# Twelve groups of experts for nine: by request, in pairs, the emptiest last

## What is computed

```
g_idx = argmax(h @ rg_w + rg_b)                      # one of 4 groups per token
e_sel = (h @ re_w + re_b)[group g_idx]               # 8 logits
top_p, top_i = top_k(softmax(e_sel), 2)              # 2 experts per token
hid = silu(h @ w_gate[e]) * (h @ w_up[e]) * combine  # 1024 -> 256
y  += hid @ w_down[e]                                # 256 -> 1024
x   = layer_norm(alpha * x + g2 * y)
```

## Time and profile before

| | us |
|---|---|
| runs shown | 1051.68, 1734.73, 1049.01 |
| median | 1051.68 |
| the profiled execution | 1051.29 |
| its span | 1049.2 |
| TensorE busy | 845.7 (81 %) |
| VectorE busy | 303.8 (29 %) |
| ScalarE busy | 176.7 (17 %) |
| moved from and to memory | 324.48 MB |

### The profile page before, as it was taken

The page is one execution under the profiler, slowest core; times in us unless marked ns, Lnnn a source line. Parts: engine busy times, 40 slices in busy tenths (PEclk is TensorE's granted clock), DMA queues, the critical chain, the costliest instruction groups (busy, mean ns, idle before and its releaser), DMA issues.

```text
span 1049.2 us, 13222 instructions
## 1 busy us (share of the span) xinstructions
PE 845.7 (81%) x5572; PEld 576.2 (55%) x5572; DVE 303.8 (29%) x674; ACT 176.7 (17%) x387; POOL 26.4 (3%) x50
## 2 busy tenths in 40 slices
PE   4899999998976985766649998998998599576572
PEld 1787757876853542322428886687886245232251
DVE  2111333222567121100052223232356712111015
ACT  2101323210122110100021033151002212010001
POOL 0200000000000000000010000000000000000000
PEclk9899999999979998877679999999998999888777
DMA  9947963586648999999995415676554899999991
GB/s 371 411 181 283 374 241 126 221 282 247 280 192 329 429 429 431 430 430 427 422 425 231 171 34 202 279 281 241 161 241 170 328 430 429 428 430 430 429 421 75
DMA packets 38519, 324.48 MB, mean 309 GB/s; under 512 B 4921, under 2 KB 5049, under 8 KB 9393
## 3 DMA queue, kind: packets, MB, share of 16 engines
q1 hardware_dynamic: 34816, 313.02, 72.5%
q0 software_dynamic: 3200, 9.09, 2.7%
q10 hardware_dynamic: 432, 1.40, 0.3%
HBM read 321.06 MB, written 2.42 MB: 308 GB/s over the span
## 4 chain that ended last, share of the span: by engine, by line
PE 66%; DMA 21%; DVE 6%; issue 3%; ACT 3%; SPq 1%; DVEq 0%; ACTq 0%
DMA expert_gate_up<-in_w_gu 19%; PE ps L852 13%; PE ps L734 9%; PE ps L760 6%; PE ps L1012 5%; PE ps L926 5%; PE ps L998 5%; PE ps L663 4%; PE ps L684 2%; DMA dense<-in_w_ada 2%; PE ps L873 2%; PE ps L822 2%; PE ps L963 2%; PE ps L704 2%; PE ps L953 2%
## 5 line engine op out<-in xcount | busy, mean ns | idle before, releaser
L852 PE MATMUL ps<-expert_gate_up,gathered_even 128*32 128x512 f32 x640 | 85.3, 692 | 48.8 <-DMA expert_gate_up<-in_w_gu 45.3
L734 PE MATMUL ps<-hT,dense 128*128 128x256 f32 x512 | 114.8, 383 | 0.0
L734 PEld LDWEIGHTS ps<-hT,dense 128*128 128x128 f32 x512 | 96.6, 191 | 15.7 <-issue 2.6
L852 PE MATMUL ps<-expert_gate_up,gathered_odd 128*32 128x512 f32 x512 | 65.2, 667 | 44.5 <-DMA expert_gate_up<-in_w_gu 44.5
L852 PEld LDWEIGHTS ps<-expert_gate_up,gathered_even 128*32 128x32 f32 x640 | 26.4, 126 | 104.1 <-issue 104.1
L760 PE MATMUL ps<-dense,hT 128*128 128x256 f32 (+1 forms) x320 | 68.1, 377 | 1.7 <-ACT hT L1124 1.7
L663 PE MATMUL ps<-dense,cond 128*32 128x256 f32 x768 | 56.0, 422 | 16.7 <-ACT cond L1217 12.3
L852 PEld LDWEIGHTS ps<-expert_gate_up,gathered_odd 128*32 128x32 f32 x512 | 20.3, 121 | 88.6 <-issue 88.6
L873 PE MATMUL ps<-expert_down,hiddenT 128*32 128x512 f32 x576 | 65.5, 594 | 2.3 <-ACT hiddenT L1188 2.3
L1585 DVE TENSOR_TENSOR hidden<-hidden,ps 128x256 f32<-128x256 f32 x18 | 7.6, 420 | 203.3 <-ACT hidden L1184 203.3
L760 PEld LDWEIGHTS ps<-dense,hT 128*128 128x128 f32 x320 | 59.9, 198 | 10.0 <-ACT hT L1124 2.5
(11 more groups left out here) (239 smaller groups left out, 1031.2 us busy)
## 6 DMA issues: line engine op xcount, KB each, us to landing
expert_gate_up<-in_w_gu SPq DMA_DIRECT2D x64, 2048.0 KB, 19.0
expert_down<-in_w_dn SPq DMA_DIRECT2D x64, 1024.0 KB, 21.2
dense<-in_w_ada SPq DMA_DIRECT2D x48, 1024.0 KB, 9.8
dense<-in_w_in SPq DMA_DIRECT2D x28, 1024.0 KB, 11.6
dense<-in_w_o SPq DMA_DIRECT2D x8, 1024.0 KB, 6.2
dense<-in_w_out SPq DMA_DIRECT2D x8, 1024.0 KB, 4.8
dense<-in_w_c SPq DMA_DIRECT2D x4, 1024.0 KB, 28.4
dense<-in_w_uq SPq DMA_DIRECT2D x4, 576.0 KB, 6.4
```

Source lines behind the costliest of these rows:

```text
L734: last = mm(b[:, m * 256:(m + 1) * 256], w[:, k, m * P:(m + 1) * P], hT[:, k, :], start=(k == 0), stop=(k == KD - 1))
L852: last = mm(ps[32 * j:32 * j + 32, bank, :], xg[n % 2][:, k, at_ + j * CAP:at_ + (j + 1) * CAP], w_gu[BUFFER[held[j]]][:, k, :], start=(k ...
```

## The change

- Twelve groups. Experts 0 to 3 go by request: group 0 has their slots for request 0, group 1 for request 1, each 32. Groups 2 to 7 take two experts each with 64 slots: 4 to 7 by number and the eight fullest of the sort. Groups 8 to 11 take the sixteen emptiest with 32 slots. Buffers 0 to 3 are therefore free after group 1.
- Group 0's input is gathered from the normalised tokens `xh2` in one float32 product and modulated on the way out (`gathered_first`); `gate_up` of groups 0 and 1 is cut into pieces of the inputs that stand between router, count and token transposes. Group 0 goes as far as its `down` and `scatter` before the loop.
- The sort is a small permutation matrix `perm` made from 64 rows; TensorE applies it (`order_experts`, `turn_route`, `sort_route`). The 24 by 24 grids are gone.
- `choose` and `place` of request 0 stand on VectorE ahead of the layer norm's second half of request 1.
- The down load of expert 5 is issued right behind its gate/up load.
- The branch to the extra rounds is behind group 9, with groups 10 and 11 to follow. The last group's `gate_up` is done in halves, two experts and then two.

```diff
-FIRST_OF = (0, 4, 8, 10, 12, 16, 20, 24, 28)
+TILES = ((0, 1, 2, 3), (0, 1, 2, 3), (4, 4, 5, 5), (6, 6, 7, 7), (8, 8, 9, 9), (10, 10, 11, 11), (12, 12, 13, 13),
+         (14, 14, 15, 15), (16, 17, 18, 19), (20, 21, 22, 23), (24, 25, 26, 27), (28, 29, 30, 31))
-GROUPS = 9
-SPLIT = 7
+GROUPS = 12
+SPLIT = 9
 ...
+                for e in (6, 7):
+                    main_load(l, e)
                 sp.wait_ge(order_ready, l + 1)
+                    for e in (8, 9):
+                        main_load(l, e, which[e - 8])
+                    for e in (6, 7):
+                        main_down(l, e)
+                    for e in (8, 9):
+                        main_down(l, e, which[e - 8])
+                for g in range(5, SPLIT + 1):
+                    next_experts(l, TILES[g][0], TILES[g][-1] + 1)
 ...
+                pe.wait_ge(*reached(m, "sel_ready", 1))
+                pe.wait_ge(xh2_ready, 2 * l + 1)
+                gather_first(m, 0)
+                ada(l, a0 + 3)
+                turn_hidden2(l, 1)
+                gate_up(m, None, 0, 4, range(0, 2))
                 router(l, 1)
+                gate_up(m, None, 0, 4, range(2, 4))
+                gate_up(m, None, 0, 4, range(4, 6))
+                count(l, 1)
+                gate_up(m, None, 0, 4, range(6, 8))
+                gather_first(m, 1)
+                evacuated(l, ("h2T", 1, 0), ("h2T", 1, 1), ("route", 1), ("count", 0), ("count", 1))
+                turn_tokens(l, 0)
+                gate_up(m, None, 1, 1, range(0, 4))
+                turn_group(m, 0, 0, 4)
+                totals(l)
+                gate_up(m, None, 1, 1, range(4, 8))
+                turn_tokens(l, 1)
+                select_T(m, 0, 5)
+                down(m, None, 0, 0, EARLY_BANK)
+                order_experts(l)
+                select_T(m, 1, 0)
+                scatter(m, 0, 0, True)
 ...
+                        if g == GROUPS - 1:
+                            gate_up(m, None, g, g % 2, held=(0, 1))
+                            gate_up(m, None, g, g % 2, held=(2, 3))
+                        if g != SPLIT + 1:
+                            scatter(m, g - 1, g - 1, g == 2)
+                    if g == 2:
+                        turn_route(l)
 ...
+                    if g == 2:
+                        sort_route(l)
+                        pe.wait_ge(sorted_ready, l + 1)
                     down(m, None, g, g)
```

More of the change, by code:

```diff
@@ L83, with experts, requests, scattered @@
 COLUMN_PARTS = {0: 0, 1: 1, 3: 2, 4: 3}
-def tiles(g):
-    a = FIRST_OF[g]
-    return [a, a, a + 1, a + 1] if g in PAIRS else list(range(a, a + EPI))
+def experts(g):
+    return sorted(set(TILES[g]))
+def requests(g):
+    return ((0,), (1,), (0, 1))[min(g, 2)]
+def scattered(g):
+    return g if g < 2 else 2 * (g - 1)
 def dense_ada(layer):
@@ L498, in main_down, with next_experts @@
                 down_load(l, M[l], e, which)
-            def four_experts(l, a):
+            def next_experts(l, first, end):
                 with ExitStack() as hold:
[L503 to L508, removed]
+                    which = [whose(hold, e) for e in range(first, end)]
+                    for e in range(first, end):
+                        main_load(l, e, which[e - first])
+                    for e in range(first, end):
+                        main_down(l, e, which[e - first])
             def extra_loads(l, r):
@@ L800, in gather_first @@
-            def gather_first(w, s):
[L802 to L810, removed]
+                        last = tr(ps[:, TOKEN_BANK[c], j * P:(j + 1) * P], h2T[:, s, 4 * c + j, :], ident)
@@ L812, in gather @@
+            def gather_first(w, s):
+                for f in range(2):
+                    for j in range(4):
+                        k = 4 * f + j
+                        last = mm(ps[:, FIRST_BANK[s][f], j * P:(j + 1) * P], xh2[:, s, k * P:(k + 1) * P],
+                                  sel[:, 0, s, 0:P].bitcast(F32), start=True, stop=True)
+                    last.then_inc(w["xg_filled"], 1)
             def gather(w, n, banks, evacs):
[L814 removed]
@@ L862, in turn_group, with down @@
                 last.then_inc(w["hidT_filled"], 1)
-            def down(w, r, done, g):
-                held = tiles(g)
-                for e in sorted(set(held)):
+            def down(w, r, done, g, banks=(2, 3)):
+                for e in experts(g):
                     pe.wait_ge(*reached(w, "dn_in", landed(r, e), BUFFER[e]))
@@ L1606, in extra_round @@
                 w = X[l]
-                first, end = PLACES_OF[WIDE]
-                for a, b, slots in ((0, first, CAP), (first, end, 2 * CAP), (end, NE, CAP)):
-                    last = V.tensor_scalar(posx[:, :, a:b], posx[:, :, a:b], -float(slots), None, ALU.add)
+                for n in range(CHUNKS):
+                    a, b = PLACES_OF[n]
+                    last = V.tensor_scalar(posx[:, :, a:b], posx[:, :, a:b], -float(SLOTS_OF[n]), None, ALU.add)
                 last.then_inc(w["round_ready"], 1)
@@ new lines, in _ @@
+                sort_experts(l)
+                weigh(l, 1)
+                select_T(m, 0, 0, 5)
+                hidden_product(m, 1, 1, 1)
+                bias_ada(7 if l == 0 else 11)
+                token_low(l, 1)
+                name_experts(l)
+                low(m, 0, 0, EARLY_BANK)
+                combine(l, 1)
+                select_T(m, 1, 1, 0)
+                select(m, 1, (0, 1))
+                if l == 0:
+                    columns(7)
+                for g in range(1, GROUPS):
+                    n = g // 2
+                    if g > 1:
+                        hidden_product(m, g, g, g % 2)
+                    if g == 2:
+                        turn_route(l)
+                    more = g % 2 and g < GROUPS - 1
+                    if more and g != SPLIT:
```

438 lines of the change are left out of this document (232 added, 206 removed).

## The result

The changed kernel takes 1061.77 us (median of 4 runs, 1060.09 to 1065.48), the kernel before 1051.62 (median of 4 beside it, one of which took 1734.73 us and stands alone). The ratio is 1.0107, 95 % interval 1.0079 to 1.0135: slower by 1.1 %, clear of no change, though by less than 2 %. 1062 was forecast. The profiled execution is the slowest of the four, 1065.48 with a span of 1063.5; before it was 1051.29 and 1049.2.

A forecast was written before the change was run, and what follows sets the result against it. TensorE was to bound the row of pair groups up to group 6, then memory after a dry queue. A later restart (3.1 us) and 203.6 us behind it gave +3.6 and +7.3 a layer: about 1062 us, range 1038 to 1077.

The forecast's parts named there:

- the sum: Both layers' expert stages added up: +3.6 us in the first, +7.3 in the second, together +10.9 on the profiled 1051.29.
- 44 MiB behind expert 18's buffer: Loads left at group 6's gate/up end, held by SP's in-order issue until its buffers are free: 107.3 us of memory time.
- The restart: Moment the expert loads resume after running dry; predicted at 328.1 us, 3.1 later than before, when group 1's gate/up ends.
- half clock: TensorE at half rate for 9 us, as in the old profile's 300 to 309 us; without it the sum is 8.4 us less.
- the walk: Engine lists followed from the first router's end (290.8 us) to group 1's gate/up end: 323.9 us at full clock.
- R: Restart of the loads in the kernel before, when group 0's gate/up ends: 325.03 us, in the second layer 826.80.
- R': Restart in the changed kernel, the end of group 0's and 1's gate/up; predicted at R + 3.1.
- Branch hidden: Tail: group 10's late start behind the branch costs nothing, its gate/up needing 15.8 us of the 19.5 before the queue empties.
- Halves bring nothing: Last group's gate/up in halves gains nothing, since `down` waits for its own weights, 9.8 us behind the last gate/up weights.
- One: Rival: the queue never runs dry, as pairs take TensorE under 29.3 us or six buffers bridge it; 1045 us, chance 0.20.
- Two: Rival: slow clock through both first groups up to group 2, 15 us more a layer; 1092 us, chance 0.15 with like stalls.
- Three: Rival: an expert gets more tokens than its slots and an extra round is run; chance under 1 in 100.

The follow-up runs named there:

- Experiments one: Changed kernel with gate/up and down loads of experts 16 to 23 issued by twos instead of fours: 1053.25 us, ratio 1.0032 to the kernel before.
- two: Kernel before with the loads of experts 16 to 23 issued by twos, a control: 1051.39 us, ratio 0.9999.
- three: Changed kernel with the low part of the gathered tokens left out of every gather but that of groups 0 and 1: 1044.61 us, ratio 0.9936.
- six: Changed kernel with `combine` of request 1 moved on VectorE ahead of `name_experts` and the first low part: 1053.79 us, ratio 1.0034.
- five: Changed kernel with the last group's gate/up in one piece instead of halves: 1062.1 us, ratio 1.0098.
- seven: Changed kernel with both loads of experts 16 to 23 by twos and `combine` of request 1 earlier: 1049.2 us, ratio 0.999.
- eight: Changed kernel without the branch and the extra rounds: 1059.2 us, ratio 1.0078.
- eleven: Kernel before with the branch behind group 5 instead of group 7, and the last gate/up in halves: 1043.11 us, ratio 0.9941.
- experiment ten: Kernel before with only the branch moved, behind group 5 instead of group 7: 1044.26 us, ratio 0.9945.

## Why the prediction was right, and where its terms were off

The forecast was 1062 and the median 1061.77. The mechanism earned the direction and the main term; that the total fits to 0.3 us is luck, for errors of some 3 us in several terms had opposite signs. In the profiled run, the slowest of the four, they didn't quite cancel: the last `down` comes 14.4 us later, for 10.9 in the sum.

**The mechanism was right.** It said that six pair groups in a row make TensorE the bound up to group 6, that SP's order then holds 44 MiB behind expert 18's buffer, and that the stage ends at this point plus the memory's time. All three are in the profile after: 70.4 us from group 2's start to group 6's end for 70.7 predicted, the issue that stretches over 19.03 us, the traffic dips at 415 and about 450 us (415 and 452 predicted). Experiments one (fill the hole: 8.5 less) and two (no hole: nothing) show that the hole costs time; three and six show that TensorE's time up to group 6 is paid in full.

**The restart was off: it came earlier than I took.** I took half clock for nine us and 3.1 us of delay. The clock from 300 to 309 us was 1.00. The transposes started at 300.17 (300.4 predicted) and the wait for `place_behind` was 2.04 (2.2), so the walk itself held; but the restart came at 325.4, R + 0.4, and in the second layer level with the time carried over from the first. Six further profiles of kernels with the same work up to there have it at 320.7 to 324.3, and 328.1 lies outside of all of them. Part of that spread is older than the routing, so I count from the end of the output projection (289.1 us before the change, 289.0 after it). The prediction's two values are then 34.8 us at full clock and 39.0 with the half clock. Of the fourteen restarts in the seven profiles nine came after 34.8 us, four after 36.4 and 36.5, one after 37.9: the walk at full clock was exact, and the half clock that I added was the step that was wrong. The clock from 309 to 321 us was 0.86 in the first layers with 36.5 and 37.9 and 1.00 in the other five, so it varies from run to run. The old order is no steadier: in the first layers of its six profiles the restart comes after 35.8 to 40.2 us. The Trainium skill's rule (TensorE: Matmul & The Clock Gate, Part 1), weighed in the prediction, spoke for the full clock, and in the stretch where I had set it aside the profile bears it out: 1.00. The time by it, 8.4 us less than the forecast, would still have been too low, for the next two reasons.

**What lies behind the restart was too short by 3 to 4 us a layer**, and that made up for the restart. The parts of the stage in every profile of the changed kernel and its variants, first layer and second, in us:

| kernel | R' to group 2 | group 2 to group 6's end | from there to the last `down` |
|---|---|---|---|
| predicted | 20.4 | 70.7 | 112.5 |
| changed | 22.0, 21.8 | 70.4, 70.4 | 115.2, 114.4 |
| one, order of the loads | 19.3, 20.3 | 70.4, 70.4 | 110.2, 112.3 |
| three, shorter gather | 18.8, 17.3 | 66.6, 66.6 | 112.1, 114.6 |
| five, last in one piece | 19.3, 20.8 | 70.4, 70.4 | 116.0, 115.2 |
| six, `combine` earlier | 17.6, 17.6 | 70.4, 70.4 | 115.4, 114.3 |
| seven, one and six | 17.6, 17.6 | 70.4, 70.4 | 113.4, 113.7 |
| eight, no branch | 20.7, 21.7 | 70.4, 70.4 | 115.7, 115.4 |

From R' to group 2 the 20.4 is in the middle of what the kernels with full gathers and the late `combine` show (19.3 to 22.0); the changed kernel's profile has it at 22.0 and 21.8 because the wait for `combine` is followed by a slow clock there, and the gather takes 5.35 for the 3.83 that I took from the earlier trace rows. The term that was too small in every profile with full gathers and the change's order of loads is the last one. The 44 MiB need 107.3 us at the rate of the rows, so some 7 to 8 us go to a start of the loads from an empty queue and to the second dip, for the 5.2 in the sum (2.7, 2.1 and 0.4). The first layer then gives +4.9 for +3.6, the second's experts +7.3 for +7.3.

**A term was missing.** The dense part of the second layer took 2.3 us more, and I had written it off as hidden. Across the profiles it varies from 243.1 to 246.4 us. The range is much the same with the old groups and the new, but over 245 us it is in five of the seven profiles with the new and in one of the six with the old. Whether that is chance or the change's doing was not tried.

**The tail.** "Branch hidden" was nearly right: 2.6 us, where it had been 9. The prediction's sign for it, no wait behind the branch that ends in anything but weights, did not come: the branch (5.31) and the gather behind it stand in the chain, and group 10 starts without waiting for weights. It cost little because the loads went on meanwhile, 423 to 427 GB/s. "Halves bring nothing" was not contradicted (experiments five and eleven), though up to some 2 us a layer would be inside the noise. `down` waits for its own weights in the second layer (0.97 us), in the first it starts within 0.3 us of the time at which they are due.

**The rivals.** One, the queue never dry, needed TensorE ahead of the loads: it was not, at group 6. With the order of experiment one the queue is nearly full, and yet the kernel takes 1053.25, not the 1045 that I gave it: group 2 starts late, and TensorE stays the bound until group 6. Two, the slow clock throughout, didn't come; short pieces of it did, from 331 to 341 us in the changed kernel's profile. Three had no case: 64 loads of each kind are on the page.

**Where the gain went.** Moving the branch is worth 7 us in the kernel before (experiment ten). The changed kernel stands 17.5 above that: mending the dry queue's order takes away 8.5, mending the wait at `combine` with the clock behind it 8.0, both 12.6. What the last 5 are (1049.2 and 1044.26) was not taken apart.

**Open:** how much of the differences of 1 to 3 us between single profiles is the clock's chance; whether the 2.3 us between the layers belong to the change; where the 2.6 us of experiment eight come from. Not tried were the early loads of experts 4 and 5 alone, the sort back on VectorE, and `choose` behind the layer norm.

## What to carry to other kernels

Where one engine issues loads in program order, the first one that must wait for a buffer holds all behind it: put the loads that can already go ahead of it (8.5 us here, for a loop by twos). When work is regrouped, compare the engine's time for what frees a set of buffers with the loads' time for the same set, over the whole stretch, gathers included; 31.5 against 29.3 us looks harmless, but over a row of such groups that began 20 us behind the restart the queue ran dry. A branch with a fixed stall belongs where the next group's weights are late anyway.

## What the runs showed of the hardware

A short wait can cost nearly its own length again in clock, but not each time: in the changed kernel's profile the 2.82 us at 331 us are followed by scatter products of 0.63 us each for 0.40, gather products of 0.41 for 0.28 and a granted clock of 0.66 over ten us, 0.9 and 1.5 us in all. With 0.85 us in its place the clock was 1.00 in all four cases; but behind the same 2.82 us it was 1.00 too in the first layer of experiment five, and in three of ten cases altogether. And the mean clock is no measure of a kernel: it rose from 0.91 to 0.95 while the time rose by 1.1 %.
